# Hybrid diffusion trunk step: fourteen conditioning blocks for the first group of the SSD scan, side work of the second input projection in another order, and the first modulated tile rounded directly

## The reference

```python
for i in range(DEPTH):                                    # DEPTH = 2
    shift, scale, gate (x2) = silu(cond) @ w_ada[i] + b_ada[i]   # "conditioning": 6 x 1024 columns, 2 condition vectors
    h = x * (1 + scale) + shift                           # "modulated" input
    if i == 0: m = ssd_mixer(h)                           # h @ w_in, conv3, silu, chunked scan, rms_norm, @ w_out
    else:      m = gdn_mixer(h)                           # h @ w_in, conv3, silu, l2 norms, delta-rule scan, @ w_out
    x = layer_norm(alpha * x + gate * m)
    f = (silu(conv3x3(h2 @ w_up[:, :FF])) * (h2 @ w_up[:, FF:])) @ w_down
    x = layer_norm(alpha * x + gate2 * f)
```

## Time and profile before

| | before |
|---|---|
| time of the runs | 1675.33, 1672.10, 1666.63 us; median 1672.1 |
| the profiled execution | 1669.27 us, span 1667.5 us |
| TensorE busy | 1559.7 us (94%) |
| ScalarE, VectorE, GpSimd busy | 781.7, 867.5, 907.3 us |
| mean granted clock of TensorE | 0.974 of full |
| weights and states read | 196.44 MB |

### The profile page before, as it was taken

One profiled execution on the slowest core, in us unless ns is written; L12 is line 12 of the kernel. 1 busy time (PEld: TensorE's weight loads), 2 busy tenths in 40 slices (PEclk: granted clock), 3 DMA queues, 4 the chain that ended last, 5 costly groups with the idle time before them and its releaser, 6 DMA issues.

```text
span 1667.5 us, 31001 instructions
## 1 busy us (share of the span) xinstructions
PE 1559.7 (94%) x11823; PEld 1478.5 (89%) x11823; DVE 867.5 (52%) x1804; ACT 781.7 (47%) x1390; POOL 907.3 (54%) x516
## 2 busy tenths in 40 slices
PE   4999998999898999999899999989888999999997
PEld 2899996777798999999899989878778989999996
DVE  0633203666536777713632447688785246777423
ACT  1654435676335444424745563534535255544323
POOL 1455555676472555557145556677735554555552
PEclk9999998999999999999999999989988999999998
DMA  8334444887551344434133332000002443444430
GB/s 326 105 117 126 128 128 149 287 293 276 197 155 51 126 126 126 154 118 146 51 127 110 98 96 89 15 27 15 13 27 96 132 126 89 126 126 130 140 122 38
DMA packets 55410, 205.38 MB, mean 123 GB/s; under 512 B 6145, under 2 KB 6145, under 8 KB 54913
## 3 DMA queue, kind: packets, MB, share of 16 engines
q1 hardware_dynamic: 54144, 201.70, 37.0%
q10 hardware_dynamic: 1152, 2.10, 0.3%
HBM read 196.44 MB, written 7.34 MB: 122 GB/s over the span
## 4 chain that ended last, share of the span: by engine, by line
PE 73%; issue 10%; DVE 7%; ACT 6%; POOL 3%; DMA 2%; POOLq 0%; DVEq 0%; SPq 0%; ACTq 0%
PE ps L747 6%; PE ps L745 6%; PE ps L746 6%; PE ps L654 5%; PE ps L656 5%; PE ps L655 5%; PE ps L2610 4%; PE ps L988 4%; PE ps L990 4%; PE ps L2612 4%; PE ps L2611 4%; PE ps L989 4%; POOL wlo L318 3%; ACT seg_lo L1154 2%; DMA raw<-w_ada_in 1%
## 5 line engine op out<-in xcount | busy, mean ns | idle before, releaser
L318 POOL TENSOR_TENSOR wlo<-raw,whi 128x1024 fp32r<-128x1024 f32 (+1 forms) x195 | 494.3, 2536 | 449.4 <-ACT whi L306 449.1
L306 ACT ACTIVATE whi<-raw 128x1024 fp32r<-128x1024 f32 (+1 forms) x241 | 265.6, 1103 | 535.2 <-PE ps L656 183.6
L745 PE MATMUL ps<-hhi,whi 128*128 128x384 f32 x656 | 219.8, 335 | 2.5 <-POOL wlo L318 2.0
L747 PE MATMUL ps<-hhi,wlo 128*128 128x384 f32 x656 | 219.2, 334 | 0.0
L746 PE MATMUL ps<-hlo,whi 128*128 128x384 f32 x656 | 219.1, 334 | 0.0
L819 DVE SCALAR_TENSOR_TENSOR evac<-ps,vec,evac 128x189 f32<-128x189 f32 (+3 forms) x440 | 166.5, 412 | 99.3 <-ACT evac L760 69.7
L2396 POOL TENSOR_TENSOR wlo<-raw,whi 128x1024 fp32r<-128x1024 f32 x46 | 110.8, 2409 | 130.9 <-ACT whi L306 130.9
L988 PE MATMUL ps<-hhi,whi 128*128 128x384 f32 x392 | 133.3, 340 | 11.0 <-DVE hlo L450 10.3
L2610 PE MATMUL ps<-hhi,whi 128*128 128x384 f32 x368 | 131.7, 358 | 3.8 <-POOL wlo L2396 3.8
L990 PE MATMUL ps<-hhi,wlo 128*128 128x384 f32 x392 | 131.9, 337 | 0.0
L989 PE MATMUL ps<-hlo,whi 128*128 128x384 f32 x392 | 131.9, 336 | 0.0
(11 more groups left out here) (340 smaller groups left out, 3538.3 us busy)
## 6 DMA issues: line engine op xcount, KB each, us to landing
raw<-w_in_in SPq DMA_DIRECT2D x98, 512.0 KB, 3.5
raw<-w_ada_in SPq DMA_DIRECT2D x96, 512.0 KB, 4.8
raw<-w_up_in SPq DMA_DIRECT2D x88, 512.0 KB, 3.5
raw<-w_down_in SPq DMA_DIRECT2D x32, 704.0 KB, 4.1
raw<-w_out_in SPq DMA_DIRECT2D x32, 512.0 KB, 3.6
s<-s_ssd_in SPq DMA_DIRECT2D x8, 256.0 KB, 4.7
o_ssd_out<-st_sb ACTq DMA_DIRECT2D x8, 256.0 KB, 2.1
S<-s_gdn_in SPq DMA_DIRECT2D x4, 512.0 KB, 3.6
```

The costliest lines, as they stand in the source:

```text
L306: act.activation(whi[:, z.mod(SPL), 0:p.kt * P], raw[:, b.mod(RAW), 0:p.kt * P], ACT.Copy).then_inc(hi_ready, 1)
L318: pool.tensor_tensor(wlo[:, z.mod(SPL), 0:p.kt * P], raw[:, b.mod(RAW), 0:p.kt * P], whi[:, z.mod(SPL), 0:p.kt * P].bitcast(F32), ALU.subt ...
L745: pe.matmul(out, a, hhi[:, k, :], start=(k == 0), stop=False)
L747: mm = pe.matmul(out, b, hhi[:, k, :], start=False, stop=(k == DT - 1))
```

## The change

Four edits. (1) The 80 conditioning blocks are dealt out as 14, 10, 10, 10, 9, 9, 9, 9. Of the first group's fourteen, six go in pairs behind the three `turn_rows` at the scan's start, two between `segment(0)` and `segment(1)`, and six inside the group; the first waits for the last gate tile, which uses the same PSUM bank. (2) In the norms, ACT writes tile 0 rounded into `hhi` straight from `xr` and then once more to PSUM; the `hlo` subtraction waits for both. (3) In the projections `run_begin(0)` moves from j = 1 to j = 2, and for n = 0 the eight RMS products are made when each tile is due: tiles 0, 1, 2 before their additions, 3 to 7 before that of tile 3. (4) In `gdn_in` block 5 is split at s = 2 between `conv_centre` and `silu` instead of at s = 3; `norm_x` runs at s = 3 to 10; `turned(0, 0)` one step later; for the next head group the decay rows go from 46 to 44, products and segments from 46 and 47 to 45 and 46, `decay_exp` from 48 to 47.

```diff
@@ norm_dve
             def low(t):
+                dve.wait_ge(h_mod, DT * m + t + 1)
                 dve.wait_ge(h_hi, DT * m + t + 1)
@@ norm_act
                 h = modulated(n, t)
+                if t == 0:
+                    for a, b, c in SEQS:
+                        i = act.activation(hhi[:, t, a:b], xr[:, t, a:b], ACT.Identity,
+                                           bias=ada[:, lay, part * DT + t, c:c + 1],
+                                           scale=ada[:, lay, (part + 1) * DT + t, c:c + 1])
+                    i.then_inc(h_hi, 1)
                 for a, b, c in SEQS:
                     i = act.activation(h[:, a:b], xr[:, t, a:b], ACT.Identity,
...
-                act.wait_ge(h_mod, DT * m + t + 1)
-                act.activation(hhi[:, t, :], h, ACT.Copy).then_inc(h_hi, 1)
+                if t:
+                    act.wait_ge(h_mod, DT * m + t + 1)
+                    act.activation(hhi[:, t, :], h, ACT.Copy).then_inc(h_hi, 1)
@@ back_act
-                if j == 1:
+                if j == 2:
                     run_begin(act, n, 0)
@@ back_dve
                 dve.wait_ge(rms_std, 1)
-                for t in range(DT):
-                    row(dve, dve.scalar_tensor_tensor(xr[:, t, :], ps[:, 7, 0:TOK], ALPHA, xr[:, t, :], ALU.mult, ALU.mult))
...
             def added(t):
                 x, o = xr[:, t, :], ps[:, t % 2, 0:TOK]
+                if n == 0 and t < 4:
+                    for q in (t,) if t < 3 else range(3, DT):
+                        row(dve, dve.scalar_tensor_tensor(xr[:, q, :], ps[:, 7, 0:TOK], ALPHA, xr[:, q, :], ALU.mult, ALU.mult))
@@ SSD scan
-        ADA_G = tuple(10 * g for g in range(SSD_G)) + (ADA_2,)
+        ADA_G = (0, 14, 24, 34, 44, 53, 62, 71, ADA_2)
...
             for c in range(NCH):
                 turn_rows(c)
+                if c == 0:
+                    pe.wait_ge(gate_done, 20)
+                conditioning(0, 2 * c, 2 * c + 2)
             segment(0)
+            conditioning(0, 6, 8)
             for g in range(SSD_G):
                 u = 3 * g
                 segment(u + 1)
                 last = g + 1 == SSD_G
                 states(g)
-                conditioning(g, 0, 2)
+                if g:
+                    conditioning(g, 0, 2)
                 entry_decays(g, 0)
                 outputs(u)
-                conditioning(g, 2, 5 if last else 4)
+                if g:
+                    conditioning(g, 2, 5 if last else 4)
+                else:
+                    conditioning(g, 8, 10)
                 turn_rows(u + 3)
                 segment(u + 2)
                 entry_decays(g, 1)
-                conditioning(g, 5 if last else 4, 8 if last else 6)
+                if g:
+                    conditioning(g, 5 if last else 4, 8 if last else 6)
+                else:
+                    conditioning(g, 10, 12)
                 entry(g, 0)
                 turn_rows(u + 4)
-                conditioning(g, 8 if last else 6, 10 if last else 8)
+                if g:
+                    conditioning(g, 8 if last else 6, 10 if last else 8)
                 outputs(u + 1)
                 turn_rows(u + 5)
                 if g + 1 < SSD_G:
                     segment(u + 3)
                 entry(g, 1)
-                if g + 1 < SSD_G:
+                if g == 0:
+                    conditioning(g, 12, 14)
+                elif g + 1 < SSD_G:
                     conditioning(g, 8, 10)
                 outputs(u + 2)
@@ gin_pool
-                if s == 46:
+                if s == 44:
                     decay_rows(pool, 1, 0)
@@ gin_act
-                if HEAD + 2 <= s + 2 < N_IN:
+                if HEAD + 3 <= s + 2 < N_IN:
                     split_hi(act, gin, Idx(s + 2))
                 if 0 <= t < CONV_T:
                     conv_centre(t)
+                if s == 2:
+                    split_hi(act, gin, Idx(HEAD + 2))
                 if 1 <= t <= CONV_T:
                     silu(t - 1)
...
-                if 1 <= s <= DT:
-                    norm_x(act, 1, s - 1, slice(s - 1, s))
+                if 3 <= s < 3 + DT:
+                    norm_x(act, 1, s - 3, slice(s - 3, s - 2))
...
-                if s == 48:
+                if s == 47:
                     decay_exp(act, 1, 0)
@@ gin_pe
                 if s == 27:
                     pe.wait_ge(l_done, 2 + 4)
                     products(pe, 0, 0)
+                if s == 28:
                     turned(pe, 0, 0)
...
-                if s == 46:
+                if s == 45:
                     pe.wait_ge(g_ktok, 1)
                     products(pe, 1, 0)
-                if s == 47:
+                if s == 46:
                     segments(pe, 1, 0)
```

## The result

Six runs of the changed kernel have a median of 1660.41 us (1655.34 to 1662.84), six of the kernel before 1670.54 (1666.63 to 1675.33): a ratio of 0.9934, interval 0.9916 to 0.9951, so 11.0 us less (8.2 to 14.0, the ratio times 1670.5). The forecast was 1659.0 in a range of 1652 to 1667, faster by over 0.5%. The profiled execution after took 1661.76 us, span 1660.0, mean granted clock 0.969 (before 1669.27, 1667.5 and 0.974).

What follows compares the result with a forecast made beforehand. TensorE, busy 94% of the span, was taken as the bound, its idle and half-clock time to be won. Terms 4.0 + 1.3 + 1.35 + 0 + 4.2 + 1.3 = 12.15 from mean 1670.8 gave 1658.7, predicted 1659, range 1652 to 1667.

Steps and rivals of the forecast that it cites:

- Part 1a: Scan's start and first group: early conditioning blocks and fuller clock gain 4.0 us, bounds 2.4 and 5.0.
- 2.31 us left the clock alone at 799: Norm 1's wait, taken as evidence that a 2.3 us wait at the scan's start would leave the clock at full.
- first rival: Scan's start and `gdn_in`: clock falls and late loads take the start back, leaving 7.2 us gained, 1663.6; chance 0.22.
- third rival: Scan's start: ACT's chain sets it too, early blocks only carried, gain there 1.0 us, total 1662; chance 0.10.
- Part 1b: Scan's later groups: one block less in four groups gains 1.3 us, 1.0 in the last; bounds 0.5 and 2.5.
- Part 3: `ssd_out`: TensorE's wait before block 4 goes, 1.35 us gained, bounds 1.0 and 1.6; other projections 0.
- Part 2: Three norms' first modulated tile: TensorE starts 0.5 us earlier but tile 1 is late next; 0 us gained.
- Part 4a: Start of `gdn_in`: block 5's wait goes, 2.3 us returns at block 6; 4.2 us gained, bounds 2.9 and 4.9.
- 3.2 us gained: `gdn_in` up to block 6: block 6 starts 3.2 us earlier than its assumed old start of 832.28.
- Part 4b: End of `gdn_in`: 2.49 us wait before `turned` goes, 1.28 table load returns; 1.3 gained, bounds 0.8 and 2.5.
- second rival: More than the sum: half clock after `rate_sums` in `gdn_in` (3.4 us) and later groups' weight waits go, 1654; chance 0.13.
- rival of a slower clock in the GDN scan: GDN scan: shifted start brings clock falls of 25 us more, cancelling the 12 us gain, 1671; chance 0.05.

Runs made afterwards that it cites:

- filler: Kernel before plus eight extra conditioning products, overwritten, where the change has its early eight; real blocks unmoved: 1668.92 us, ratio 0.9997.
- six-block deal: Changed kernel with ten conditioning blocks in groups 1 to 6 and six in the last: 1657.64 us against the kernel before's 1669.49, ratio 0.9934.
- repeat: The changed kernel run again, unaltered, beside the kernel before: 1659.87 us against 1670.14, ratio 0.9942.
- edit 3: Kernel before with only `run_begin(0)` moved later and the eight RMS products made when due: 1667.86 us, ratio 0.9992.
- edit 1 with ten blocks: Kernel before with eight early conditioning blocks but ten in every group, two of the first group's left inside it: 1668.32 us, ratio 0.9993.
- edit 2: Kernel before with only the norms' first modulated tile rounded straight from `xr`: 1669.86 us, ratio 0.9991.
- edit 4a: Kernel before with only the start of `gdn_in` changed, block 5 split ahead of silu and `norm_x` two steps later: 1667.80 us, ratio 0.9990.
- edit 1: Kernel before with only the new dealing and early places of the conditioning blocks: 1664.51 us against 1669.07, ratio 0.9967.
- edit 4b: Kernel before with only the end of `gdn_in` changed, the scan's first products a step earlier and `turned(0, 0)` one later: 1668.92 us against 1669.49, ratio 1.0006.

## Why the prediction was right, point by point

**Part 1a, 4.0 us forecast: the moved work came out as forecast, the clock did not; 2.2 on average.** The gap of 2.3 before the second `turn_rows`, the missing one before the third, the earlier `states` and the row copy that follows (286.77 where "near 285" stood) are all there. The pair that no longer stands behind `states` (1.0) and the shorter group (0.6) were to give 1.6, and the last column of the table above gives 1.8. The step that failed is the clock: the other 2.4 of the 4.0 stood on "2.31 us left the clock alone at 799", which is one execution. Here the same gap had a fall within 1 us of its end in six of seven executions, and the stretch up to the end of `states` became 0.3 us shorter on average. In norm 1 itself, with that wait as before, four of seven profiles had the clock at half for 6.8 us around it. So the first rival was right in part, and one sign of being wrong, "a clock of 0.50 at the start", was there; so was a gap for weights before `segment(1)`, of 0.23 us here and up to 1.12 in the siblings. The "3.4 to 4.7 us" that I took as the usual landing was short: 4.7 is the median of the 79 loads from 240 to 440 us in the kernel before. The one execution with the clock at 1.00 throughout, 29.86, is near what the upper end described: 4.2 us below the kernel before's own 34.02. The third rival (the early blocks only carried, 1.0) is nearer than I gave it credit for, with 1.8 instead of 1.0.

**Part 1b, 1.3 us: right in size, 1.4 on average, shared out otherwise.** The later groups gained 2.4 us in the pair of profiles, against 0.3 forecast; but the five without the edit have 120.89, 119.34, 118.57, 118.51 and 119.33, and the four with this dealing 118.5: 0.8 on average. Most of the 2.4 was weights that came late in the one profiled execution of before. TensorE's waits from 240 to 440 us after, in the columns of the earlier trace rows:

```profile
PE ps L388 <- DMA raw<-w_ada_in: 3.2, 5, 1.5
```

instead of 5.5 in 8. The last group, for which I had counted 1.0, gained nothing in the pair and 0.6 on average: the block went, and the waits moved to the blocks that were left. Six blocks there show that it is bound by its loads, and that the next bound lies right behind it.

**Part 3, 1.35 us: right for the gap, and the stage gained more.** The gap went, 1.4 to 1.6 us with what came off block 2, and nothing took its place. DVE's later products stayed hidden. `ssd_out` and norm 0 together have a mean of 95.4 us in the six profiles without the edit (the filler left out) and 92.5 in the four with it and nine or ten blocks in the last group: 2.9 less. The other 1.5 is half clock in norm 0 that came in only one of them, a term that the forecast doesn't have.

**Part 2, 0: right.** TensorE starts 0.5 us earlier in a norm and pays it at tile 1; at full clock the stretch from the last sums to the next stage's first own block is 18.1 us without the edit and 18.2 with it. TensorE's timeline of norm 1, in the kernel with three things reordered on ScalarE, where the clock was full:

```profile
790.48 0.41 PE L351 MATMUL ps<-hhi,head_hi 128*128 128x384 f32 x1 [1.82 <-ACT hhi L618]
...
791.95 0.79 PE L355 MATMUL ps<-hlo,head_hi 128*128 128x384 f32 x3 [0.18 <-DVE hlo L577]
```

The gap is 1.82 instead of 2.31, and `hlo` is now waited for, for 0.18. What I had not seen is that this stretch, too, is one where the clock falls in some executions: the 1.71 us that norm 1 lost in the profile after are that.

```profile
794.27 0.52 PE L352 MATMUL ps<-hhi,head_lo 128*128 128x384 f32 x1
```

A product of 0.33 us takes 0.52 there. Before, at full clock, it took 0.34. Such falls came in norm 1 in four of the seven profiles without the edit and in two of the six with it, so they come without it too. The edit alone has 0.9991 with 1 inside its interval; that it makes them more or less likely isn't shown.

**Part 4a, 4.2 us: the order was right and the size wrong, 2.3 in the trace and 1.7 (at most 3.7) in the runs.** "3.2 us gained" is the first step that was off. I set the old start of block 6 at 832.28, adding 0.64 for the sum product; it had started at 831.99. And ScalarE ended block 6's rounding 0.4 us later than in my walk through it, and `wlo` was 0.1 later again. That leaves 18.43 - 16.09 = 2.34. Then I added 1.0 for a fall of the clock that would not recur: in both profiled executions of the changed kernel, and in that with the six-block deal, it did recur, one block later, after the gap of 2.56 us. The first rival said so ("the 2.3 us wait brings a fall too"), and was right in this part; the one execution of the edit alone in which it stayed up shows that it need not. Removing the gap removed the fall, and was worth 3.7 us by the medians and 3.9 in the trace: 2.6 up to block 6 and the rest, 1.1 to 1.3, behind it, somewhat less than the 1.7 that 3.4 us at half clock would cost.

**Part 4b, 1.3 us: about 0.7 in the trace, none in the runs.** The step "POOL's decay rows two steps earlier delay one `wlo` by at most 0.2 us, not seen by TensorE" was wrong. POOL after:

```profile
1018.93 2.49 POOL L2110 TENSOR_TENSOR gr<-masks,small 128x512 f32<-128x512 f32 x2
1021.38 2.83 POOL L2419 TENSOR_TENSOR wlo<-raw,whi 128x1024 fp32r<-128x1024 f32 x1
```

Two decay rows take 2.49 us and not 2.04, the `wlo` behind them 2.83 and not 2.41, and it ends at 1024.2, 0.7 after TensorE was free. On the table load, where "ScalarE: Activation LUTs" of the Trainium skill (What ACT_TABLE_LOAD costs) would have added a drain of 1.38 us to each switch, the rows go on showing none: the load of 1.28 at 1048.88 starts as the activation before it ends (1048.27 and 0.60) and is followed by its own at 1050.18. That part came out at nothing all the same, but by the 0.71 and the 1.1 above, not by the drain.

**Why the total was right.** In part by terms that erred both ways. Taken against the siblings' means, 1a was too large by 1.8, 4a by 1.9 and 4b by 0.6, 4.3 us in all; the fall in norm 0 that mostly stayed away gave back 1.5 and 1b 0.1. 12.15 less 4.3 and plus 1.6 is 9.5, close to the repeat (9.7) and the sum of single edits (9.0). The 11.0 of these six runs lie 1.3 above the repeat, within the intervals: that is chance, and so is that the forecast missed by only 1.4 us. The second rival's other half did occur in the profiles: after `rate_sums` the clock was at half for 3.4 us, not 6.8. The other kernels had 6.8 (before, edit 3, edit 1 with ten blocks), 3.4 (edit 2, edit 4a, and all five with the whole change in them) or 0 (edits 1 and 4b, filler), a mean of 3.4 us without edit 4a and with it. So this is luck against the one profile of before, and not the change. The rival of a slower clock in the GDN scan shows in the rows, at a size too small to decide: 227.42 to 229.08 between the two profiles, and, as said under edit 4b, 1.4 us between the means with and without that edit.

What stays open is what decides whether such a gap brings the clock down. The same gap of 2.56 was followed by 0.55 in the changed kernel, 0.56 in its repeat, 0.50 with the six-block deal, and 1.00 with the edit alone.

## What to carry to other kernels

When an edit takes a wait away, walk each engine to the next block and price what is late next; here that found the new gap within 0.3 us, and the further reordering that removes it was worth 2.2 to 3.7 us more, no less than the first. Weigh each stage against several executions before giving it a gain: a pair of profiles had stages with little or no edit that differ by 1.7 to 2.4 us, the size of most terms. Cut such a stage once more, where the clock stops mattering: the part behind `states` gave 1.8 us in all but one of the profiles (2.3 there), while the part ahead of it varied by 3. And an engine that looks idle between its large pieces (POOL here, with 1.5 to 2.4 us between two `wlo`) has no room for 2.5 us of small work ahead of the next one.

## What the runs showed of the hardware

The granted clock differs from execution to execution, in places and in length, where the code is the same: after `rate_sums` it was at half for 0, 3.4 or 6.8 us, at the scan's start without edit 1 for 10.2 or 13.7 and with it for 0, 3.4 or 6.8, and over the whole span for some 66 to 110 us in the thirteen profiles (from mean granted clocks of 0.980 over 1652.3 us and 0.967 over 1665.2). The spread is not small beside a change of this size: 31 runs of the kernel before on one chip lie between 1664.27 and 1677.16. A gap of 2.31 us left the clock at 1.00 before one norm and at one start of the scan, and was followed by 0.50 at 261.4 in the changed kernel; one of 1.82 stayed at 1.00. "TensorE: Matmul & The Clock Gate" of the Trainium skill (HAM oscillation) describes bursts between waits for loads that each run cold. The waits of its example are longer than these, so it does not follow from them that the start would gain its lower bound. In these traces the clock was at half within 1 us of the end of a wait of 2.3 to 2.6 us in most executions (six of seven at the scan's start, three of four in `gdn_in`) and at full in the others.
